# Gate products of the mixer issued three at a time, and put between the small products of the GLA heads' outputs

## Reference, cut to what matters

```python
h = z @ w_in
(q_a, k_a, v_a, r_a, lr_f, lr_b, q_b, k_b, v_b, g_a, g_b) = jnp.split(h, SPLIT_POINTS, axis=-1)
a = gla_branch(q_a, k_a, v_a, r_a, lr_f, lr_b, gla_w2, gla_b2, gla_gn)      # 4 heads
b = attention_branch(q_b, k_b, v_b, q_norm, k_norm, cos, sin)              # 8 heads
y = (jax.nn.sigmoid(g_a + b_merge[0]) * (a @ w_pa)
     + jax.nn.sigmoid(g_b + b_merge[1]) * (b @ w_pb))
```

## Time and profile before

| | |
|---|---|
| median of 3 runs | 2732.22 us (2731.74 to 2734.68) |
| the profiled execution | 2732.64 us, of which the profile's span is 2730.7 us |
| TensorE busy, mean granted clock | 2502.7 us (92%), 0.963 of full speed |
| woven part, layer 0 | about 306.6 to 450 us of the span |
| woven part, layer 1 | about 1002 to 1111 us of the span |

### The profile page before, as it was taken

The page is one execution under the profiler, slowest core; times in us unless marked ns, Lnnn a source line. Parts: engine busy times, 40 slices in busy tenths (PEclk is TensorE's granted clock), DMA queues, the critical chain, the costliest instruction groups (busy, mean ns, idle before and its releaser), DMA issues.

```text
span 2730.7 us, 47823 instructions
## 1 busy us (share of the span) xinstructions
PE 2502.7 (92%) x19338; PEld 2067.9 (76%) x19338; DVE 1054.1 (39%) x2380; ACT 887.7 (33%) x1488; POOL 1057.9 (39%) x437
## 2 busy tenths in 40 slices
PE   7999999999999989999987899999888779999997
PEld 7998878999999887899987555555577675555554
DVE  3413734543442283544074332322226443232323
ACT  4434423444443353344432122121124522122121
POOL 6874523788788463578773000000034320000000
PEclk9999979999999999999998999999988989999999
DMA  7545512454554532355565899999853149999996
GB/s 240 176 149 142 170 32 93 155 177 155 178 186 149 135 139 76 108 170 166 178 165 214 326 422 421 421 421 421 358 173 117 36 198 407 421 421 421 421 421 255
DMA packets 287884, 644.09 MB, mean 236 GB/s; under 512 B 35584, under 2 KB 209792, under 8 KB 238336
## 3 DMA queue, kind: packets, MB, share of 16 engines
q1 hardware_dynamic: 284672, 635.79, 62.9%
q10 hardware_dynamic: 2176, 3.15, 0.5%
q0 software_dynamic: 896, 3.15, 0.4%
HBM read 637.85 MB, written 4.19 MB: 235 GB/s over the span
## 4 chain that ended last, share of the span: by engine, by line
PE 77%; DMA 10%; DVE 9%; ACT 2%; issue 1%; SPq 0%; POOL 0%; DVEq 0%; ACTq 0%
PE bank L582 39%; DMA wring<-in_exp_w 10%; PE bank L1110 7%; PE bank L1088 6%; PE bank L546 5%; PE bank L681 4%; PE bank L1121 3%; PE bank L1067 3%; PE bank L1080 3%; PE bank L615 1%; PE bank L759 1%; DVE ARENA L1973 1%; PE bank L834 1%; DVE XN_rounded L1570 1%; PE bank L556 1%
## 5 line engine op out<-in xcount | busy, mean ns | idle before, releaser
L2030 POOL TENSOR_TENSOR wring_rounded<-wring,wring_rounded 128x1024 fp32r<-128x1024 f32 (+1 forms) x400 | 1029.7, 2587 | 564.0 <-ACT wring_rounded L1181 563.5
L582 PE MATMUL bank<-SQ_rounded,wring_rounded 128*128 128x272 f32 (+1 forms) x3968 | 744.7, 288 | 28.7 <-POOL wring_rounded L2030 17.7
L582 PEld LDWEIGHTS bank<-SQ_rounded,wring_rounded 128*128 128x128 f32 x3968 | 624.4, 190 | 32.0 <-POOL wring_rounded L2030 13.7
L582 PE MATMUL bank<-XN_rounded,wring_rounded 128*128 128x272 f32 (+1 forms) x1984 | 569.4, 287 | 0.0
L1181 ACT ACTIVATE wring_rounded<-wring 128x1024 fp32r<-128x1024 f32 (+1 forms) x400 | 441.7, 1106 | 353.3 <-PE bank L582 346.8
L582 PE MATMUL bank<-ARENA_rounded,wring_rounded 128*128 128x272 f32 (+1 forms) x3456 | 434.8, 288 | 13.3 <-DVE ARENA L1737 4.2
L582 PEld LDWEIGHTS bank<-ARENA_rounded,wring_rounded 128*128 128x128 f32 x3456 | 430.1, 191 | 17.3 <-DVE ARENA L1737 4.4
L582 PEld LDWEIGHTS bank<-XN_rounded,wring_rounded 128*128 128x128 f32 x1984 | 377.0, 190 | 0.2
L1470 ACT ACTIVATE ARENA<-bank 128x512 f32<-128x512 f32 x128 | 76.4, 597 | 671.8 <-PE bank L1110 671.8
L1110 PE MATMUL bank<-wring,ARENA 128*32 128x512 f32 x2048 | 246.2, 598 | 40.4 <-DVE ARENA L1973 30.3
L1088 PE MATMUL bank<-ARENA 64*128 64x256 f32 x2048 | 255.7, 389 | 1.6 <-ACT ARENA L1462 1.6
(11 more groups left out here) (241 smaller groups left out, 2321.2 us busy)
## 6 DMA issues: line engine op xcount, KB each, us to landing
wring<-in_exp_w SPq DMA_DIRECT2D x256, 1024.0 KB, 17.9
ARENA<-in_exp_w SPq DMA_DIRECT2D x128, 1024.0 KB, 16.5
wring<-in_ffn_w_gate SPq DMA_DIRECT2D x44, 1024.0 KB, 5.5
wring<-in_ffn_w_up SPq DMA_DIRECT2D x44, 1024.0 KB, 8.1
wring<-in_ffn_w_down SPq DMA_DIRECT2D x32, 1408.0 KB, 6.2
wring<-in_w_in SPq DMA_DIRECT2D x14, 2048.0 KB, 7.9
wring<-in_conv_w_in SPq DMA_DIRECT2D x24, 512.0 KB, 5.4
wring<-in_attn_w_in SPq DMA_DIRECT2D x5, 2048.0 KB, 7.7
```

Of the source, the lines that this page charges most:

```text
L582: ins = nc.tensor.matmul(o, rounded(a_[:, k, cols]), rounded(x), start=(start and k == 0 and j == 0), stop=(stop and k == len(tiles) - 1 a ...
L2030: st.done(nc.gpsimd.tensor_tensor(rounded(low), low, part(high), ALU.subtract), wl_ready)
```

## The change

The generator gives way after each `k`, so that it issues eighths of 3 matmuls. In steps without a head's output two eighths go where one quarter went, and the order is as before. In a step with a head's output one eighth goes between `scores` and `turn_rows` and one between `turn_rows` and `values`, and the other eighths of the step (2 to 6) go into `head_out`, behind the claim of bank 7: every so many products an eighth, and what is left after the last. No matmul is added or taken out, and the programs of the other engines stay as they are.

```diff
--- before.py
+++ after.py
@@ -667,7 +667,7 @@
                 if (l, j) != (0, 1):
                     column_means(7, "mean_d", rows(SQ, n)[KD - 2:], "act", KD - 2)
 
-            def gate_quarters(n):
+            def gate_eighths(n):
 
                 for g in range(16):
                     b = GATE_BANKS[g % 2]
@@ -680,7 +680,7 @@
                         for j, (a_, x) in enumerate(((low, SQ), (high, XN), (high, SQ))):
                             ins = nc.tensor.matmul(bank[b][:, 0:n], rounded(a_[:, k, :]), rounded(x[:, k, 0:n]),
                                                    start=(k == 0 and j == 0), stop=(k == KD - 1 and j == 2))
-                        if k in (1, 3, 5):
+                        if k < KD - 1:
                             yield
                     chunk_done(ins, bank_full["act"][b])
                     held[b] = "act"
@@ -691,7 +691,12 @@
                 plan_ = WOVEN[l]
                 units, nq = plan_.units, plan_.n
                 st.need(zn_ready, KD)
-                gates = gate_quarters(nq)
+                gates = gate_eighths(nq)
+
+                def weave(n):
+                    for _ in range(n):
+                        next(gates)
+
                 v = cols_of(("in3", l), 304)
                 products(KEY_BANK, "act", "dve",
                          [[(bank[KEY_BANK][:, 0:T], v[:, k, 48:176], x) for k, x in enumerate(rows(XN))]])
@@ -729,8 +734,7 @@
                 for b in R_BANKS:
                     split_products(b, "act", pairs(SQ, XN, KD, nq))
 
-                for _ in range(QUARTERS_FIRST):
-                    next(gates)
+                weave(2 * QUARTERS_FIRST)
                 st.need(d2p)
                 def scores(n):
                     h, t = units[n]
@@ -810,7 +814,7 @@
                                        VA[r0:r0 + nr, t, h * P:h * P + P])])
                     products(WOVEN_BANK, "dve", "dve", g)
 
-                def head_out(h, r0):
+                def head_out(h, r0, gate_parts):
                     hp, by_row = 64 * (h % 2), {0: [], 64: []}
                     tile = slice(h // 2 * P, h // 2 * P + P)
                     if r0 == 0:
@@ -830,7 +834,11 @@
                         by_row[hp].append((o, ST[hp:hp + 64, 1, 3, tile], QD[hp:hp + 64, 1, h // 2, SEQ:T]))
                     if r0 == 64:
                         pe.wait_ge(*lower_rows[h])
+                    every = max(len(by_row[r0]) // max(gate_parts, 1), 1)
                     for i, (o, l_, r_) in enumerate(by_row[r0]):
+                        if gate_parts and i % every == every - 1:
+                            weave(1)
+                            gate_parts -= 1
                         ins = nc.tensor.matmul(o, l_, r_, start=(r0 == 0 and i == 0),
                                                stop=(r0 == 64 and i == len(by_row[64]) - 1), skip_group_check=True)
                     if r0 == 0:
@@ -839,6 +847,7 @@
                     else:
                         st.done(ins, bank_full["act"][WOVEN_BANK])
                         held[WOVEN_BANK] = "dve"
+                    weave(gate_parts)
 
                 def head_means():
                     st.need(sq_ready, 4)
@@ -848,18 +857,21 @@
                 lower_rows = {}
                 scores(0)
                 for n in range(plan_.steps):
-                    quarters = plan_.quarters[n]
+                    left = 2 * plan_.quarters[n]
+                    outs = (n + 1 in plan_.outs) + (n in plan_.outs)
+                    share = 1 if outs else 2
                     if n + 1 < len(units):
                         scores(n + 1)
-                    next(gates)
+                    weave(share)
                     if 1 <= n <= len(units):
                         turn_rows(n - 1)
-                    if quarters > 1:
-                        next(gates)
+                    between = min(share, left - share)
+                    weave(between)
                     if n >= 2:
                         values(n - 2)
-                    for _ in range(2, quarters):
-                        next(gates)
+                    left -= share + between
+                    if not outs:
+                        weave(left)
                     if n == plan_.keys[0]:
                         st.need(gla_ready)
                     if n in plan_.keys:
@@ -871,9 +883,9 @@
                     if n in plan_.states:
                         states(plan_.states.index(n))
                     if n + 1 in plan_.outs:
-                        head_out(plan_.outs.index(n + 1), 0)
+                        head_out(plan_.outs.index(n + 1), 0, left if outs == 1 else 0)
                     if n in plan_.outs:
-                        head_out(plan_.outs.index(n), 64)
+                        head_out(plan_.outs.index(n), 64, left)
                     if n == plan_.mean:
                         head_means()
```

## The result

The changed kernel takes 2774.03 us (median of 4 runs, 2767.41 to 2777.64) against 2733.45 (2731.74 to 2734.98): ratio 1.0148, 95% interval 1.0128 to 1.0168, slower by 40.6 us. The forecast was slower, 2759.5 us in a range of 2741 to 2775. The direction was right, and the size was 14.5 us short: the median lies 1 us inside the end of the range and outside the forecast's own 2752 to 2767.

A forecast was written before the change was run, and what follows sets the result against it. TensorE was taken as the bound, busy 92% of the span, so only its time per matmul and its clock counted. Terms 6.5 + 8.1 + 12.7 = 27.3 us on 2732.6, less 0.4 for the median, gave 2759.5; range 2741 to 2775.

The forecast's parts named there:

- the forecast's own 2752 to 2767: Range for the main case, layer 0 at half clock and layer 1 as before; chance 0.48.
- Term 1: Head steps of both layers: 37 further gate runs cost entries, 8.1 us in layer 0 at half clock, 6.5 in layer 1.
- Term 2: Layer 0's head steps: clock stays at half until steps 19 and 20, costing 12.7 us on steps 16 to 19.
- the spell at 394: Layer 0's short full-clock spell near 394 us, expected to remain; losing it too would cost 2.8 us more.
- the pattern of six gates, three transposes, six gates: Layer 0: absent from the eight changed steps, so the clock was expected at half until steps 19 and 20.
- Layer 1's clock: Layer 1's head steps: 27.3 us from 1070 left at full clock, no term; if not, up to 22 us.
- the prediction's own sign: Layer 1's part from step 10 on would be about 6.5 us longer if the forecast was right.
- rival 4: Layer 1's clock falls as well, for half of its 27 us: 11 us more, 2770; chance 0.2.
- Waits: Bank 7's claim ahead of the eighths in head steps: nothing to 1 us, taken as nothing; step 13's 3.1 us wait stays.
- (1): Full clock holds in layer 0's head steps, gaining 15.3 us there: 2728 us; chance 0.1.
- (2): Entries into further gate runs are free and the clock holds: 2715 us; chance 0.04.
- 3: Layer 0's clock rises as early as before or several times: 2747 to 2750 us; chance 0.18.

The follow-up runs named there:

- the second experiment: Changed kernel, but eighths for a head's output stand in one run behind bank 7's claim, ahead of its products; 2739.45 us, ratio 1.0002 to 1.0042 against the kernel before.
- experiments 9: Order of the kernel before, with products of the heads' outputs over 128 rows in place of 64 (does not compute the reference's result); 2722.52 us, ratio 0.9965 to 0.9999.
- experiment 10: Changed kernel's order, with products of the heads' outputs over 128 rows in place of 64 (does not compute the reference's result); 2725.68 us, ratio 0.9968 to 1.0005.
- the first experiment: Changed order in layer 0 only, layer 1's head steps in the order of before; 2757.0 us, ratio 1.0068 to 1.0132 against the kernel before.
- experiments 3: Changed kernel, but a whole quarter stays on each side of the transposes in head steps, only the remainder goes between products; 2743.12 us, ratio 1.0022 to 1.0066.
- 7: Changed kernel, but eighths inside a head's output go in two at a time, at half as many places; 2762.21 us, ratio 1.0090 to 1.0140 against before.
- 11: Changed kernel, but gate matmuls inside a head's output go in one at a time in place of three; 2814.57 us, ratio 1.0271 to 1.0325 against before.
- experiment 5: Changed order in layer 1 only, layer 0 in the order of before; 2750.81 us, ratio 1.0054 to 1.0102 against the kernel before.
- experiments 4: Changed kernel with products of the heads' outputs over 128 rows in place of 64 (does not compute the reference's result); 2729.8 us, ratio 0.9974 to 1.0029 against before.

## Why the prediction was right, and where it was short

**Term 1, the further runs: right.** 36 and 39 runs stand in the trace. At full clock a run costs 0.36 us (forecast 0.34). At half clock step 15 of layer 0 took 14.98 us in the changed kernel and 13.52 in the second experiment, both at half throughout: 1.46 us for 3 runs, 0.49 each (forecast 0.45). So 18 x 0.49 = 8.8 and 19 x 0.36 = 6.9 us, where 8.1 and 6.5 were forecast. That the change of shape is what costs is shown by experiments 9 and 10. (Not all 37 further runs begin behind a head's product, as the prediction has it: 34 more than before do, by the trace. It changes no term.) By "TensorEngine Tiling (Array Packing)", Key Properties, in the Trainium skill, a changed tiling mode drains the engine; the runs agree and add the price.

**Term 2, layer 0's clock: right in kind, its size within the scatter.** Part 0 lost 24.5 us, less 8.8 for the runs is 15.7; the forecast was 12.7, with the bound of 2.8 more "if the spell at 394 is lost too". It was lost in this execution, and not in the first experiment's, which has the same order in layer 0. The fall came at 374.9 us (forecast: about the same time), the half clock ended at 463.7 (past 430). Against the profiles on record part 0 lost between 18 and 30 us (85.9 less 67.7, 92.2 less 62.3), so that 12.7 comes near is in part luck.

**Its reason was partly wrong.** The forecast had the rise hang on the pattern of six gates, three transposes, six gates. Experiments 1 and 2 rose without it. The kernel before, which the prediction was made from, has it at 379.07 us without a rise, and the changed kernel has it in step 19 (451.95 us) and came back only in step 20. Both times a wait of TensorE follows soon (3.1 and 2.2 us). What the kernels show together is a trend: with the same gates and heads, the mean clock goes down as runs are added. (The order of before has 0.72 and 0.80 in part 0 and 0.90 to 0.97 in part 1. Part 0: 0.81, 0.67, 0.62, 0.54, 0.55 with 2, 6, 8, 18 and 50 further runs in experiments 3, 2, 7, the changed kernel and 11. Part 1: 0.90, 0.77, 0.88, 0.82, 0.54 with 1, 9, 10, 19 and 32 in experiments 2, 7, 3, the changed kernel and 11.) The order is not strict. In part 1 experiments 3 and 7 add nearly as many runs, and the one that keeps whole quarters around the transposes has 0.88 and 51.6 us, the other 0.77 and 57.3. So the dense pattern goes with a higher clock, though single profiles do not prove it. The exact condition was not found.

**Layer 1's clock: this is the step that failed.** The 27.3 us at full clock from 1070 were left at full, with "no term". It measured 12.2 - 6.9 = 5.3 us in the profile, and the prediction's own sign, a part "about 6.5 us longer", came out as 12.2. The clock had fallen just ahead of the head steps in both kernels (1063.1 and 1091.7 us). Before, it rose at 1070.0, behind two whole runs of gates around the transposes of step 10. Now step 10 goes on with six eighths and six products in turn at half clock, and it came back at 1112.2. This is no accident of one profile: with the changed order the stretch lasted 20.5 us in experiment 5 too, with the order of before 3.4 to 10.2 us. The price was named, as rival 4, "for half of its 27 us", with 0.2, and not put in the sum. I had argued from how dense a product with an eighth is at full clock. The part starts at half clock in both kernels, and the question there is what brings the clock back.

**Waits: right.** Bank 7's claim held TensorE once for 3.1 us in both kernels, though it stands ahead of the eighths now. No other wait in the head steps is longer than before's.

**The rest.** 8.8 + 15.7 + 6.9 + 5.3 is 36.7 us. The spans differ by 39.1. Of the other 2.4, 1.8 lie between the first gate matmul of layer 0 and step 11, where the order is the same; 1.3 of them are a wait for ACT's gate tile (line 1294 now) that the other profile has not. Against the forecast the terms came out 0.7, 3.0, 0.4 and 5.3 us higher and this rest 2.4: every slip has the same sign, and nothing was made up by another. How much of the 40.6 us is the clock is known for the profiled executions only: about 21 of 37.

**Rivals.** The clock did not hold in layer 0 (1), and entries are not free (2): experiments 9 and 10 show what would have to be true for that, products of the gates' own shape. Layer 0 did not rise as early as before (3; by its own terms that case reaches to 2752 us, not 2750). Layer 1's clock did stay down longer (4), for 5.3 us more by the profiles where 11 were given; of all the cases priced this one, 2770 us, is the nearest to what came.

## What to carry to other kernels

Before weaving two strands of matmuls, look at their shapes: going over between 64 and 128 rows cost 0.36 us there and back at full clock, as much as three gate matmuls, and 0.49 at half, and finer weaving multiplies it; with one shape it was free. Putting dense work between the thin products did not raise the clock here, and each place where it went in cost time of its own. No version tried was faster than the kernel before while computing the same.

## What the runs showed of the hardware that was not expected

- The same pieces in the same order (scores, three gates, three transposes, three gates, values, about 5 us at half clock) brought the clock back in two kernels (395.0 us, experiment 2; 397.5 us, experiment 1) and not in another (from 395.96 us, changed). Experiment 1 and the changed kernel have the same order in the whole of layer 0, so what stands around the pieces does not decide it alone. What does is not shown.
- One kernel's single runs differ by up to 16 us (2722 to 2738 for the kernel before), and the longer ones have the lower mean clock (2721.96 us at 0.969, 2737.52 at 0.962). Part 0 of one and the same kernel differs by 8.2 us (71.3 and 63.1, experiments 4 and 10), with a mean clock of 0.70 and 0.81.
- The clock fell with TensorE busy without a break: before, in layer 0, 6.85 of 6.85 us up to the fall at 373.65.
- Products over 128 rows in place of 64, with the same columns, did not cost more in the order of before, and may have gained: the medians are 8.6 us apart (2722.52 against 2731.12), but the ratio of the runs is 0.9982, 0.9965 to 0.9999, hardly clear of none.
- A change of shape holds back weight loads too. In the changed kernel a product's first load starts 0.34 us after the load of the gate matmul before it. With products of 128 rows (experiment 10) it starts 0.12 us after it, at 1086.43 behind 1086.31. The changed kernel's:

```profile
1124.71 0.19 PEld L681 LDWEIGHTS bank<-SQ_rounded,wring_rounded 128*128 128x128 f32 x1
1125.05 0.29 PEld L842 LDWEIGHTS bank<-ARENA 64*128 64x128 f32 x2
```
